# The rounded weight pieces start 64 bytes past a multiple of 256 instead of on one

## The chip, the cores and the metric

The kernel runs on one core of one Trainium2 chip. The metric is device time in microseconds (us) of one execution. Before the change three timed runs took 3041.02, 3044.77 and 3041.26 us; the median is 3041.26 us.

## The reference

The reference is one forward pass over 512 tokens of width 1024, in float32: a first block with four kinds of attention and a feed-forward part with a short convolution, then two layers of a second block. Cut to what matters here:

```python
def first_block(x, ...):                                  # once
    x = x + token_mixer(rmsnorm(x, norm_mix_g), ...)      # proj = xn @ w_in; four attentions; gates; @ w_out
    x = x + conv_ffn(rmsnorm(x, norm_ffn_g), ...)         # xn @ w_up (1024 x 5632), conv of width 3, @ w_down
    return rmsnorm(x, norm_final_g)

for l in range(2):                                        # second block
    h = h + 0.5 * swiglu(rmsnorm_2(h, ...), w_gate, w_up, w_down)       # 1024 x 2816, 1024 x 2816, 2816 x 1024
    z = rmsnorm_2(h, mix_norm[l]) @ w_in[l]
    y_a, y_b, y_c, y_d = mla(...), spatial_gating(...), hgrn2(...), retention(...)
    h = h + concatenate([y_a, y_b, y_c, y_d]) @ w_out[l]
    h = h + 0.5 * swiglu(rmsnorm_2(h, ...), w_gate, w_up, w_down)
    h = h + (p[l] @ ple_w_proj[l]) * sigmoid(rmsnorm_2(h, ...) @ ple_w_gate[l])
return rmsnorm_2(h, final_norm)
```

By far the most work is the product of the 512 tokens with weight matrices that are read from HBM once each.

## The kernel before

**Products in three terms.** A float32 value is split into a rounded part and the rest, both stored as float32r ("fp32r" in the trace, shown as f32 with TensorE's instructions). Activations `x` become `xh` and `xl`, weights become `wh` and `wl`. A product is then three matmuls that add up in one PSUM bank: `wh` with `xh`, `wh` with `xl` (both in a first loop over the chunks of 128 along the contraction), and `wl` with `xh` (in a second loop). In `products` these are lines 728, 729 and 737; `fm_steps` has them on lines 775, 776, 780 and 784, `grains_fm` on 850, 851 and 858, the down projection of `ffn` on 1269, 1270 and 1277.

**Who is stationary.** Nearly always the weights are stationary (128x128, loaded by a LDWEIGHTS ahead of each matmul) and 512 tokens stream past them. So each float32r matmul with 512 columns has its own weight load, which runs while the matmul before it still streams. In the token-major form (`token_major` and `grains_tm`, lines 808 to 885) it is the other way round: the activations are stationary and 256 columns of `wh` or `wl` stream.

**Pieces.** Weights come in pieces of 128x1024 float32 values (`PIECE`), two slots deep. The sync engine (SP) loads piece n into `raw[:, n % 2, :]`. GpSimd (POOL) writes `wh[:, n % 2, :]` from it in one instruction (line 678) and `wl[:, n % 2, :]` as raw minus wh in four (line 685). A slot of `wh` may be written again when TensorE's first loop over the piece before last is done (semaphore `rounded_read`), a slot of `wl` when its second loop is done (`pieces_used`). TensorE waits for `pieces_split`. The activations are in `xh`, `xl`, `op_hi`, `op_lo` or in the large tensor `arena` (seen as float32r under the name `arena_rounded`).

**Where things lie.** Tensors are allocated one behind the other, each start rounded up to a multiple of 32 bytes; every number here is bytes within a partition. What TensorE reads starts so:

| tensor | start | start mod 256 | read by TensorE as |
|---|---|---|---|
| `arena` | 18432 | 0 | both operands |
| `xh`, `xl`, `op_hi`, `op_lo` | 142592, 158976, 175360, 183552 | 0 | streamed, sometimes stationary |
| `const` | 199968 | 32 | both, plain float32 |
| `ident16`, `mask16` | 204096, 204352 | 64 | both, bf16 |
| `between` | 204640 | 96 | by nobody: it fills 160 bytes |
| `wh`, `wl` | 204800, 212992 | 0 | stationary; streamed in the token-major form |
| `ones` | 221568 | 128 | stationary, plain float32 |
| `nrm` | 223104 | 128 | stationary, four matmuls |

A chunk of 128 columns of a piece is 512 bytes, and so is the step between the chunks: where `wh` starts at a multiple of 256, each stationary operand in it does too. The streamed activations also step by multiples of 512 bytes.

**Other matmuls.** The attentions and mixers use plain float32 operands. The profile has two matmuls for each plain float32 one of the program. Those matter below which follow directly on a float32r stream: line 901 (`squares`, stationary `ones`), line 1490 (`mean_square`, stationary `const`), line 1312 (`rank_one`, stationary in `arena`), and line 1122 (`qk`, stationary in `arena`).

**What sets the order.** TensorE's order is written out by hand: the matmuls of the pieces are laid between those of the attentions and mixers. Nothing in it depends on addresses.

Of the kernel before, what the change touches and what calls it, by code (L numbers as in the profile page):

```python
# [30 lines left out]
P = 128  # L31
# [208 lines left out]
def program(nc, x, out, k, scratch, book):  # L240
# [3 lines left out]
    def sb(name, shape, dt=F32):  # L244
        return ctx.enter_context(nc.sbuf_tensor(name, shape, dt))
# [29 lines left out]
    const = sb("const", [P, CONST_N])  # L275

    ident16, mask16 = sb("ident16", [P, P], BF16), sb("mask16", [P, P + 2], BF16)
    sb("between", [P, 40])
    assert nc.sbuf_base % 256 == 0, nc.sbuf_base % 256
    wh, wl = sb("wh", [P, 2, PIECE], F32R), sb("wl", [P, 2, PIECE], F32R)  # L280
    lcol = sb("lcol", [P, LAYERS * L_NROWS])
    ones = sb("ones", [P, 3, P])
# [2975 lines left out]
def build(nc, arrays, known=None):  # L3258

    k = {n: nc.dram_tensor(f"in_{n}", a.shape, mybir.dt.from_np(a.dtype), kind="ExternalInput").ap()  # L3260
         for n, a in arrays.items()}
    out = nc.dram_tensor("out_0", (1, S, D), F32, kind="ExternalOutput").ap()
    scratch = nc.dram_tensor("t5_by_distance", (8, 640), F32).ap()
    book = Book(known)
    program(nc, k["x"][0], out[0], k, scratch, book)
    return book
# [20 lines left out]
```

## Time and profile before

| | |
|---|---|
| timed runs | 3041.02, 3044.77, 3041.26 us, median 3041.26 us |
| profiled execution | 3041.56 us, its span 3040.3 us |
| mean granted TensorE clock | 0.998 of full speed |
| TensorE matmuls | 14934, busy 3003.6 us (99%) |
| TensorE weight loads | 14934, busy 2432.5 us (80%) |
| POOL | busy 2176.3 us (72%) |
| VectorE (DVE), ScalarE (ACT) | busy 1415.7 us (47%), 724.5 us (24%) |
| DMA | 272.90 MB, mean 90 GB/s |

The span is the time from the first to the last instruction of the program; the profiled execution's own time is 1.3 us longer. In the trace a matmul's record begins when it begins to stream and ends when its result is modelled to be complete, so records overlap: a duration of 389 ns does not mean that the next matmul waits for 389 ns. The distance from start to start is what a matmul costs.

### The profile page before, as it was taken

How to read it: one execution, taken by the hardware profiler on the slowest of the kernel's cores; microseconds unless marked ns; L12 is line 12 of the kernel's file. 1: busy time of each engine (PE TensorE's matmuls, PEld its weight loads, DVE VectorE, ACT ScalarE, POOL GpSimd, SP SyncE). 2: the span in 40 equal slices, each digit the busy share in tenths (PEclk: the TensorE clock that was granted, in tenths of full speed). 3: DMA queues.
4: the chain of work that ended last, by engine and by line, in shares of the span. 5: the costliest groups of instructions: out<-in, count | busy, mean ns of one | idle time of the engine just before them, and what ended most of it. 6: DMA issues, size and time to landing. Idle time of an engine off the chain costs nothing.

```text
span 3040.3 us, 39415 instructions
## 1 busy us (share of the span) xinstructions
PE 3003.6 (99%) x14934; PEld 2432.5 (80%) x14934; DVE 1415.7 (47%) x2157; ACT 724.5 (24%) x1434; POOL 2176.3 (72%) x2524
## 2 busy tenths in 40 slices
PE   9999999999999999999999999999999999999998
PEld 7776777888888888887788888888888877888886
DVE  5467556777156421476732212622213767422214
ACT  3433222222021100344411101311002444111003
POOL 6665668988788877754487777877777554877775
PEclk9999999999999999999999999999999999999999
DMA  5322223333333333322133333333323221333332
GB/s 162 79 67 63 77 80 91 97 97 97 99 100 104 97 97 97 92 55 62 56 99 97 97 103 97 94 98 97 98 96 94 63 55 54 100 97 98 104 97 83
DMA packets 469205, 272.90 MB, mean 90 GB/s; under 512 B 20798, under 2 KB 465136, under 8 KB 469016
## 3 DMA queue, kind: packets, MB, share of 16 engines
q1 hardware_dynamic: 466904, 267.22, 29.7%
q10 hardware_dynamic: 2112, 3.17, 0.3%
q8 instruction: 118, 1.93, 0.3%
q14 instruction: 71, 0.58, 0.1%
HBM read 268.21 MB, written 2.12 MB: 89 GB/s over the span
## 4 chain that ended last, share of the span: by engine, by line
PE 86%; DVE 3%; ACT 1%; issue 0%; DVEq 0%; ACTq 0%
PE bank L728 17%; PE bank L729 17%; PE bank L737 17%; PE bank L1269 7%; PE bank L1277 7%; PE bank L1270 7%; PE bank L850 2%; PE bank L858 2%; PE bank L851 1%; PE bank L775 1%; PE bank L776 1%; DVE arena L2343 1%; PE bank L780 1%; PE bank L1122 1%; PE bank L1442 1%; PE bank L885 1%
## 5 line engine op out<-in xcount | busy, mean ns | idle before, releaser
L685 POOL TENSOR_TENSOR wl<-raw,wh 128x256 fp32r<-128x256 f32 x2016 | 1617.0, 832 | 286.0 <-PE bank L737 182.2
L678 POOL TENSOR_SCALAR wh<-raw 128x1024 fp32r<-128x1024 f32 x504 | 562.8, 1117 | 555.4 <-PE bank L729 170.2
L728 PE MATMUL bank<-xh,wh 128*128 128x512 f32 x1552 | 610.7, 393 | 0.0
L729 PE MATMUL bank<-xl,wh 128*128 128x512 f32 x1552 | 604.3, 389 | 0.0
L2343 DVE TENSOR_TENSOR arena<-bank,nrm 128x512 f32<-128x512 f32 x236 | 152.4, 685 | 541.9 <-PE bank L737 541.7
L737 PE MATMUL bank<-xh,wl 128*128 128x512 f32 x1552 | 390.6, 391 | 0.0
L2343 DVE TENSOR_TENSOR arena<-arena 128x512 f32<-128x512 f32 (+1 forms) x373 | 339.1, 915 | 59.5 <-ACT arena L2059 11.7
L728 PEld LDWEIGHTS bank<-xh,wh 128*128 128x128 f32 x1552 | 291.7, 188 | 62.7 <-issue 2.1
L737 PEld LDWEIGHTS bank<-xh,wl 128*128 128x128 f32 x1552 | 289.9, 188 | 64.6 <-issue 4.6
L729 PEld LDWEIGHTS bank<-xl,wh 128*128 128x128 f32 x1552 | 291.5, 188 | 60.4 <-issue 1.2
L728 PE MATMUL bank<-arena_rounded,wh 128*128 128x512 f32 x824 | 321.7, 390 | 1.0 <-DVE arena L2343 1.0
L729 PE MATMUL bank<-arena_rounded,wh 128*128 128x512 f32 x824 | 320.6, 389 | 0.0
L2352 DVE SCALAR_TENSOR_TENSOR h<-bank,h 128x512 f32<-128x512 f32 x64 | 44.3, 692 | 481.0 <-PE bank L1277 445.9
L1269 PE MATMUL bank<-arena_rounded,wh 128*128 128x512 f32 x592 | 230.7, 390 | 0.0
L1270 PE MATMUL bank<-arena_rounded,wh 128*128 128x512 f32 x592 | 230.3, 389 | 0.0
L1991 ACT ACTIVATE arena<-arena 128x512 f32<-128x512 f32 x88 | 55.7, 633 | 682.6 <-DVE arena L2343 682.6
L737 PE MATMUL bank<-arena_rounded,wl 128*128 128x512 f32 x824 | 203.5, 389 | 0.0
L728 PEld LDWEIGHTS bank<-arena_rounded,wh 128*128 128x128 f32 x824 | 154.7, 188 | 34.0 <-DVE arena L2343 1.4
L729 PEld LDWEIGHTS bank<-arena_rounded,wh 128*128 128x128 f32 x824 | 154.7, 188 | 32.4 <-issue 0.5
L737 PEld LDWEIGHTS bank<-arena_rounded,wl 128*128 128x128 f32 x824 | 154.7, 188 | 32.1
L1277 PE MATMUL bank<-arena_rounded,wl 128*128 128x512 f32 x592 | 161.5, 389 | 0.0
L1277 PEld LDWEIGHTS bank<-arena_rounded,wl 128*128 128x128 f32 x592 | 111.1, 188 | 23.2
(370 smaller groups left out, 4098.6 us busy)
## 6 DMA issues: line engine op xcount, KB each, us to landing
raw<-in_ffn_w_gate SPq DMA_DIRECT2D x176, 256.0 KB, 3.1
raw<-in_ffn_w_up SPq DMA_DIRECT2D x176, 256.0 KB, 3.1
raw<-in_ffn_w_down SPq DMA_DIRECT2D x176, 256.0 KB, 2.9
raw<-in_w_in SPq DMA_DIRECT2D x158, 256.0 KB, 3.1
raw<-in_w_up SPq DMA_DIRECT2D x88, 256.0 KB, 3.2
raw<-in_w_gate SPq DMA_DIRECT2D x64, 256.0 KB, 3.1
raw<-in_w_out SPq DMA_DIRECT2D x48, 256.0 KB, 3.0
raw<-in_w_down SPq DMA_DIRECT2D x44, 256.0 KB, 2.9
```

The source lines that it names most:

```text
L678: pool.tensor_scalar(wh[:, s, :], raw[:, s, :], 1.0, 0.0, ALU.mult, ALU.add).then_inc(split, 1)
L685: ins = pool.tensor_tensor(wl[:, s, c], raw[:, s, c], wh[:, s, c].bitcast(F32), ALU.subtract)
L728: pe.matmul(psum, cols(wh, i), xhi, start=(i == 0), stop=False)
L729: ins = pe.matmul(psum, cols(wh, i), xlo, start=False, stop=False)
L737: ins = pe.matmul(psum, cols(wl, i), xhi, start=False, stop=(i == last))
L850: pe.matmul(o, cols(wh, i), xhi, start=(i == 0), stop=False)
L858: ins = pe.matmul(o, cols(wl, i), xhi, start=False, stop=(i == last))
L1269: pe.matmul(bank[2 * s + b][:, :], w, xhi, start=(kk == 0 and i == 0), stop=False)
L1270: ins = pe.matmul(bank[2 * s + b][:, :], w, xlo, start=False, stop=False)
L1277: ins = pe.matmul(bank[2 * s + b][:, :], cols(wl, i, b), hid[2 * kk + i][0], start=False, stop=end)
L1991: act.activation(t, t, other_table(ACT.Silu)).then_inc(*A.up("silu", tag, n))
L2343: v.tensor_tensor(out, a, b, op).then_inc(*V.up(*what))
```

## The change

The filler `between` grows from 40 to 56 float32 values, that is by 64 bytes. All that is allocated behind it moves up by 64 bytes: `wh` (now at 204864, 64 past a multiple of 256), `wl` (at 213056, likewise 64 past), `lcol`, `ones` (now 192 past a multiple of 256) and `nrm` (likewise 192 past). Nothing ahead of it moves: `arena`, `xh`, `xl`, `op_hi`, `op_lo`, `raw` and `const` stay. The instructions of every engine, their order and their waits are the same as before.

```diff
     ident16, mask16 = sb("ident16", [P, P], BF16), sb("mask16", [P, P + 2], BF16)
-    sb("between", [P, 40])
-    assert nc.sbuf_base % 256 == 0, nc.sbuf_base % 256
+    sb("between", [P, 56])
+    assert nc.sbuf_base % 256 == 64, nc.sbuf_base % 256
     wh, wl = sb("wh", [P, 2, PIECE], F32R), sb("wl", [P, 2, PIECE], F32R)
     lcol = sb("lcol", [P, LAYERS * L_NROWS])
     ones = sb("ones", [P, 3, P])
```

## Rows read from the trace of the kernel before

**Rows 1.** Page: busy time of TensorE and POOL; the chain that ended last, by line.
```profile
PE 3003.6 (99%) x14934; PEld 2432.5 (80%) x14934; DVE 1415.7 (47%) x2157; ACT 724.5 (24%) x1434; POOL 2176.3 (72%) x2524
...
PE bank L728 17%; PE bank L729 17%; PE bank L737 17%; PE bank L1269 7%; PE bank L1277 7%; PE bank L1270 7%; PE bank L850 2%; PE bank L858 2%; PE bank L851 1%; PE bank L775 1%; PE bank L776 1%; DVE arena L2343 1%; PE bank L780 1%; PE bank L1122 1%; PE bank L1442 1%; PE bank L885 1%
```
**Rows 2.** Busy by stretch: stretch, length, then busy and count for each engine.
```profile
600.00:700.00 100.00, 100.00 (x442) 82.78 (x442) 73.08 (x75) 25.74 (x37) 88.26 (x92) 1.00 0.33 96
...
1020.00:1180.00 160.00, 160.00 (x707) 132.49 (x706) 38.47 (x47) 16.38 (x26) 120.32 (x147) 1.00 0.31 96
2010.00:2280.00 270.00, 270.00 (x1193) 223.58 (x1192) 66.23 (x83) 29.00 (x46) 202.35 (x248) 1.00 0.32 96
```
**Rows 3.** L728: count, duration ns least/median/most, first and last start.
```profile
L728 PE MATMUL bank<-xh,wh x1552: 387/389/798, 51.0 to 2604.3; 128*128 128x512 f32 x194
...
L728 PE MATMUL bank<-arena_rounded,wh x824: 389/389/798, 30.8 to 3023.6; 128*128 128x512 f32 x165
...
L728 PE MATMUL bank<-op_hi,wh x112: 389/392/504, 191.0 to 2603.9; 128*128 128x512 f32 x112
```
**Rows 4.** L1269: the same view.
```profile
L1269 PE MATMUL bank<-arena_rounded,wh x592: 387/389/481, 754.9 to 2966.6; 128*128 128x512 f32 x198
...
L1269 PE MATMUL bank<-op_hi,wh x160: 389/389/389, 749.4 to 2941.2; 128*128 128x512 f32 x160
...
L1269 PE MATMUL bank<-xh,wh x128: 389/389/389, 1776.1 to 2952.1; 128*128 128x512 f32 x128
```
**Rows 5.** Groups of PE: count | busy us, mean ns | idle before.
```profile
L850 PE MATMUL bank<-xh,wh 128*128 128x512 f32 x192 | 80.1, 417 | 0.4 <-ACT arena L2092 0.4
...
L775 PE MATMUL bank<-xh,wh 128*128 128x512 f32 x96 | 37.7, 393 | 2.6 <-DVE xl L2343 2.1 <-DVE xl L2352 0.5
```
**Rows 6.** One matmul each, L780 and L851, the last ahead of L901 and L1490.
```profile
L780 PE MATMUL bank<-xh,wl x1: 396/396/396, 519.8 to 519.8; 128*128 128x512 f32 x1
```
```profile
L851 PE MATMUL bank<-xl,wh x1: 397/397/397, 2477.9 to 2477.9; 128*128 128x512 f32 x1
```
**Rows 7.** One matmul each, L737 and L851, the last ahead of L1312 and L1122.
```profile
L737 PE MATMUL bank<-xh,wl x1: 389/389/389, 2329.8 to 2329.8; 128*128 128x512 f32 x1
```
```profile
L851 PE MATMUL bank<-xl,wh x1: 389/389/389, 2471.8 to 2471.8; 128*128 128x512 f32 x1
```
**Rows 8.** Timeline of PE: start us, length us; what follows the four matmuls above.
```profile
520.04 1.02 PE L901 MATMUL bank<-arena,ones 128*128 128x512 f32 x2
```
```profile
2478.14 1.02 PE L1490 MATMUL bank<-arena,const 128*128 128x512 f32 x2
```
```profile
2329.99 0.39 PE L1312 MATMUL bank<-const,arena 128*128 128x1 f32 x3
```
```profile
2471.99 0.38 PE L1122 MATMUL bank<-arena 96*128 96x128 f32 x2
```
**Rows 9.** Timeline of PE behind a group of transposes.
```profile
293.97 0.39 PE L729 MATMUL bank<-xl,wh 128*128 128x512 f32 x1
...
295.13 0.39 PE L728 MATMUL bank<-xh,wh 128*128 128x512 f32 x1
...
296.49 0.39 PE L728 MATMUL bank<-xh,wh 128*128 128x512 f32 x1
```
**Rows 10.** L1523 and L1338, plain float32 matmuls: least/median/most ns.
```profile
L1523 PE MATMUL bank<-arena,const x16: 592/592/646, 1403.4 to 2493.0; 128*128 128x512 f32 x16
```
```profile
L1338 PE MATMUL bank<-arena,const x8: 592/592/648, 1385.0 to 2462.2; 128*128 128x512 f32 x8
```
**Rows 11.** L876, token-major: `wh` streams, 256 columns.
```profile
L876 PE MATMUL bank<-wh,xh x256: 277/283/387, 76.5 to 2499.9; 128*128 128x256 f32 x128
```
**Rows 12.** POOL's groups: count | busy us, mean ns | idle us before.
```profile
L685 POOL TENSOR_TENSOR wl<-raw,wh 128x256 fp32r<-128x256 f32 x2016 | 1617.0, 832 | 286.0 <-PE bank L737 182.2 <-PE bank L858 52.5 <-PE bank L885 29.2
L678 POOL TENSOR_SCALAR wh<-raw 128x1024 fp32r<-128x1024 f32 x504 | 562.8, 1117 | 555.4 <-PE bank L729 170.2 <-PE bank L1270 145.2 <-PE bank L877 77.9
```

## The prediction

> **What bounds the kernel now.** I read the page first, then busy time by stretch, then single lines of TensorE with their least, median and longest durations, and last the timeline around the places where float32r matmuls meet others. On the page the reader is to see that matmuls are under way for 99% of the span and that three quarters of the chain that ended last are six lines, the three terms of a product in `products` and in the down projection [rows 1]. So the end is set by how fast TensorE can begin one matmul after another. The stretches give that pace: 442, 707 and 1193 matmuls in 100, 160 and 270 us, 226 to 227 ns each, at full clock, with VectorE busy between a quarter and three quarters of the time [rows 2]. The pace does not react to VectorE. At 2.4 GHz, the clock granted there, 512 columns take 213.3 ns. So each matmul carries 13 ns beyond its columns.
>
> These 13 ns are what the change can touch, since it moves no instruction and no wait, only the address of the stationary operand of most matmuls. How many are concerned: L728 has 1552 + 824 + 112 = 2488 [rows 3], L1269 592 + 160 + 128 = 880 [rows 4], L850 192 and L775 at least 96 [rows 5]: 3656, and each has two partners (the other terms), so 10,968 matmuls with 512 columns and a weight load each. Smaller groups of the same kind, some 500, are left out. **One nanosecond more or less for each is 11.0 us, or 0.36%.** Nothing else in this kernel has such a lever.
>
> All streamed activations start at a multiple of 256 in these rows, be it in `xh` (256 past a multiple of 512) or in `arena` (0 past it). The median is 389 ns for both [rows 3, 4]: a shift of 256 between the two operands changes nothing. What a shift of 64 does no float32r row shows. I bound it.
>
> **Part 1, the stationary operand moves by 64 bytes.** The trace has one natural experiment. A weight load runs beside the matmul ahead of it. Where a float32r stream ends and a plain float32 matmul follows, the last stream runs beside a load from another tensor. Ahead of L901 (stationary `ones`, 128 past a multiple of 256) that last matmul lasts 396 ns, ahead of L1490 (stationary in `const`, 32 past one) 397 ns [rows 6, 8]. Ahead of L1312 and L1122, whose stationary operands lie in `arena` at a multiple of 256, the same kind of matmul lasts 389 ns, the median of all [rows 7, 8]. I read durations here because the end is modelled from the pace: a longer one goes with a later next start. So two offsets on either side of 64, namely 32 and 128, cost 7 to 8 ns, and offset 0 costs nothing. That is the nearest row to the change.
>
> Against taking it whole: these are single matmuls at a change of kind, not a stream in which every load is shifted. And the cost isn't a function of the addresses alone. Behind transposes the float32r stream runs with unchanged alignment, but its first matmuls come slower: from 293.97 to 295.13 are five distances, 1.16 us or 232 ns each; from 295.13 to 296.49 six, 1.36 us or 227 ns each [rows 9]. The stream finds its steady pace after some five matmuls. With the loads shifted it may settle at another pace. The unsettled distances are 5 ns over the settled ones, the shifted loads 7 ns. I take 6 ns, between the two: 10,968 x 6 = 66 us. The ends: 0 if the stream settles to the old pace, 8 ns or 88 us if every matmul pays what the one ahead of L1490 pays, 100 us if those left out pay it too; and below nothing, next.
>
> Downwards: the fastest matmuls of L728 and L1269 last 387 ns, 2 ns under the median [rows 3, 4], so -22 us is a pace that occurs. A farther bound comes from plain float32, which streams a column in two cycles: 592 ns for 512 columns [rows 10]. That is 203 ns more than 389, where the columns alone take 213.3 ns more. So a plain float32 matmul carries 10 ns less beside its load. If the shift took away all that the float32r stream has on top, it would be 10 x 10,968 = 110 us less.
>
> **Part 2, `wh` and `wl` as the streamed operand.** Token-major matmuls last 283 ns in the median, 277 at least [rows 11]; with 256 columns each, L876 and its partners L877 and L885 are 768. For a streamed operand off its place I have plain float32 only: L1338 streams from 160 past a multiple of 256, L1523 from a multiple of 256, and both have 592 ns [rows 10]. I take 0. With 8 ns each it would be 6 us, with -6 ns it would be -5 us.
>
> **Part 3, POOL.** It writes `wh` and `wl` 64 bytes farther on. One piece costs POOL 1117 + 4 x 832 = 4445 ns [rows 12]; TensorE uses a piece for 24 matmuls, 24 x 227 = 5450 ns. So 1.0 us for each piece is idle, and POOL's idle time, 286 + 555 us, is mostly ended by TensorE giving a slot back [rows 12]. Any change of under a fifth in POOL's writes stays hidden. If the cover were gone, TensorE would wait at each of the 504 pieces. `lcol`, `ones` and `nrm` move too; `ones` was off a multiple of 256 already (128, now 192). I take 0 for both.
>
> **Sum.** 3041.6 us for the profiled execution (its span 3040.3 and 1.3 around it), plus 66 us, is 3108 us. That execution is 0.3 us above the median of the runs, so I leave it at 3108.
>
> **Rival 1: nothing changes, 3041 us.** The steady pace would be the same for any shift that keeps whole lines of memory. For it: a shift by 256 does nothing, POOL and VectorE do nothing to the pace, and the stream returns to it after each disturbance [rows 2 to 4, 9]. Against: the 7 to 8 ns [rows 6]. The Trainium skill supports this rival ("TensorE: Matmul & The Clock Gate", step by step, LDWEIGHTS): the streamed operand and the weight load have two independent read ports, so a load takes no bandwidth from the running matmul. By that rule addresses could not matter, and 396 against 389 ns would have to come from something else in the change of kind, such as the two passes of a plain float32 matmul; L1312, also plain float32 with stationary operand at a multiple of 256, speaks against that. The same section gives 216 ns for bf16 matmuls of 512 columns one after another; this trace has 227 for float32r with a load each.
>
> **Rival 2: faster.** The extra 13 ns are not fixed: they differ by 5 ns with the same addresses [rows 9], so a part is two readers getting into each other's way, and plain float32 at half the rate of columns is spared 10 of them. Had the two operands started in the same place of the memory's interleaving so far, 64 bytes would pull them apart. The small form is the pace of the fastest rows, 3041 - 22 = 3019 us; the large one takes the 10 ns away, 3041 - 110 = 2931 us. Against: 32 and 128 are apart as well and cost more, not less.
>
> **Rival 3: slower by POOL.** If a shifted start broke up POOL's accesses and its instructions grew by more than 23%, POOL would set the pace: at 30% more, a piece would take 5.78 us instead of 5.45, and 504 of them 166 us more, 3207 us. Nothing in the trace speaks for it, as all starts stay at multiples of 64.
>
> **How the numbers follow.** The forecast, slower by the shifted loads, gets 0.52: two rows agree, but they are single matmuls. No change gets 0.22. Faster gets 0.24, half of it the small form, half the large one or what lies between. POOL gets 0.02. The likeliest case's own range is 3060 (2 ns) to 3145 us (the 100 us above and a few for part 2). For 8 in 10 I take 3005 to 3150: this leaves out half of the faster cases, the POOL case and little above. Under 0.2%, some 6 us, is what a measurement of this kernel can't tell from no change; on each side of it: faster 0.24, same 0.22, slower 0.54.
>
> **What would show it.** In the profile after, busy time by stretch between 2010 and 2280 us would hold 1150 to 1170 matmuls instead of 1193, and the median of L728 would be 394 to 397 ns instead of 389, that of L1523 592 as before. With rival 1 the medians stay at 389; with rival 2 they fall to 387 or to about 379. With rival 3 they stay and TensorE waits for POOL's L678 and L685. I am wrong if the stream settles: then only the matmuls behind a change of kind differ. The matmul ahead of L901 is a further test: its load moves from 128 to 192 past a multiple of 256, and ahead of L1312 a load at a multiple of 256 now runs beside a stream whose own load was shifted.

## The result and the profile after

The kernel after takes 3109.73 us in the median (3108.87 to 3111.62, four runs); the kernel before took 3041.14 us beside it (3040.90 to 3044.77, four runs). The ratio is 1.0224, with a 95% interval of 1.0206 to 1.0241: slower by 68.6 us. The forecast was 3108 us, in a range of 3005 to 3150.

The profiled execution took 3111.62 us, its span 3110.3 us, 70.0 us more than before, at a granted clock of 0.997. The page shows the same number of instructions; only TensorE's busy time has grown with the span, by 70.5 us against [rows 1]:

```profile
PE 3074.1 (99%) x14934; PEld 2433.0 (78%) x14934; DVE 1412.0 (45%) x2157; ACT 724.3 (23%) x1434; POOL 2162.8 (70%) x2524
```

The same three stretches as in [rows 2] (stretch, length, then busy time and count for PE, PEld, DVE, ACT and POOL, then the granted clock, the DMA share and GB/s):

```profile
600.00:700.00 100.00, 100.00 (x430) 80.13 (x430) 70.88 (x72) 24.89 (x36) 84.64 (x90) 1.00 0.32 95
1020.00:1180.00 160.00, 160.00 (x688) 128.92 (x687) 40.64 (x51) 16.39 (x26) 116.11 (x143) 1.00 0.31 95
2010.00:2280.00 270.00, 270.00 (x1159) 217.58 (x1158) 72.28 (x91) 29.71 (x47) 198.74 (x244) 1.00 0.32 95
```

430, 688 and 1159 matmuls stand where there were 442, 707 and 1193. That is 232.6, 232.6 and 233.0 ns for each instead of 226.2, 226.3 and 226.3, at the same full clock: 6.2 to 6.6 ns more (one matmul more or less in a count is 0.5 ns in the shortest stretch and 0.2 ns in the longest). It is so in a stretch in which VectorE is busy for 71% of the time and in one where it is 25%, so how busy VectorE is does not matter here.

The float32r lines, with least, median and longest duration, against [rows 3, 4]:

```profile
L728 PE MATMUL bank<-xh,wh x1552: 392/394/802, 50.8 to 2662.6; 128*128 128x512 f32 x194
...
L728 PE MATMUL bank<-arena_rounded,wh x824: 393/398/801, 30.6 to 3093.6; 128*128 128x512 f32 x165
...
L728 PE MATMUL bank<-op_hi,wh x112: 392/398/505, 191.7 to 2662.1; 128*128 128x512 f32 x112
```
```profile
L1269 PE MATMUL bank<-arena_rounded,wh x592: 393/394/481, 769.2 to 3035.3; 128*128 128x512 f32 x198
```

The fastest matmul of line 728 with `xh` now (392) is slower than its median was (389). Plain float32 matmuls, against [rows 10], have not moved, and the token-major ones, against [rows 11], are shorter:

```profile
L1523 PE MATMUL bank<-arena,const x16: 592/592/647, 1433.9 to 2550.2; 128*128 128x512 f32 x16
```
```profile
L876 PE MATMUL bank<-wh,xh x256: 276/279/393, 76.3 to 2557.1; 128*128 128x256 f32 x128
```

What happened is best seen where a float32r stream starts. The place of [rows 9], behind the same transposes, looks so in the timeline of the kernel after (start us, length us):

```profile
297.29 0.40 PE L729 MATMUL bank<-xl,wh 128*128 128x512 f32 x1
...
299.63 0.40 PE L729 MATMUL bank<-xl,wh 128*128 128x512 f32 x1
...
300.56 0.40 PE L729 MATMUL bank<-xl,wh 128*128 128x512 f32 x1
```

From 297.29 to 299.63 are ten distances, 234 ns each, and from 299.63 to 300.56 four, 232 ns. Before, the stream ran at 232 ns for five matmuls and then fell to 227. Now it starts near that pace and never falls: it is the pace in the middle of a long stretch too (2088.27 to 2090.14 are eight distances, 1.87 us or 234 ns each):

```profile
2088.27 0.39 PE L729 MATMUL bank<-xl,wh 128*128 128x512 f32 x1
...
2090.14 0.39 PE L729 MATMUL bank<-xl,wh 128*128 128x512 f32 x1
```

Five is not a fixed number. Behind other transposes of the kernel before, the stream needed ten distances to settle (98.14 to 100.44 us, 2.30 us or 230 ns each, and 227 to 228 from there on), and behind some only two (from 363.13 us).

```profile
98.14 0.39 PE L729 MATMUL bank<-xl,wh 128*128 128x512 f32 x1
...
100.44 0.39 PE L729 MATMUL bank<-xl,wh 128*128 128x512 f32 x1
```

POOL, against [rows 12], has more idle time than before and slightly shorter instructions:

```profile
L685 POOL TENSOR_TENSOR wl<-raw,wh 128x256 fp32r<-128x256 f32 x2016 | 1610.5, 830 | 318.6 <-PE bank L737 213.5 <-PE bank L858 53.0 <-PE bank L885 30.5
L678 POOL TENSOR_SCALAR wh<-raw 128x1024 fp32r<-128x1024 f32 x504 | 555.3, 1102 | 606.0 <-PE bank L729 201.4 <-PE bank L1270 162.8 <-PE bank L877 76.9
```

### The profile page after: what moved, and what is told of

It is laid out like the page before. It is cut to its first block, busy times and chain, and to the rows that moved or that the text cites. A ratio compares the mean times of both kernels' runs of the same rounds, so it can differ in the third digit from the quotient of the medians.

```text
span 3110.3 us, 39415 instructions
## 1 busy us (share of the span) xinstructions
PE 3074.1 (99%) x14934; PEld 2433.0 (78%) x14934; DVE 1412.0 (45%) x2157; ACT 724.3 (23%) x1434; POOL 2162.8 (70%) x2524
## 4 chain that ended last, share of the span: by engine, by line
PE 94%; DVE 4%; ACT 1%; issue 0%; DMA 0%; DVEq 0%; SPq 0%; ACTq 0%
PE bank L728 19%; PE bank L737 18%; PE bank L729 18%; PE bank L1269 7%; PE bank L1277 7%; PE bank L1270 7%; PE bank L850 2%; PE bank L858 2%; PE bank L851 1%; DVE arena L2343 1%; PE bank L775 1%; PE bank L776 1%; PE bank L1122 1%; PE bank L920 1%; PE bank L780 1%; PE bank L885 1%
## 5 line engine op out<-in xcount | busy, mean ns | idle before, releaser
L685 POOL TENSOR_TENSOR wl<-raw,wh 128x256 fp32r<-128x256 f32 x2016 | 1610.5, 830 | 318.6 <-PE bank L737 213.5
L678 POOL TENSOR_SCALAR wh<-raw 128x1024 fp32r<-128x1024 f32 x504 | 555.3, 1102 | 606.0 <-PE bank L729 201.4
L728 PE MATMUL bank<-xh,wh 128*128 128x512 f32 x1552 | 619.9, 399 | 0.0
L729 PE MATMUL bank<-xl,wh 128*128 128x512 f32 x1552 | 613.5, 395 | 0.0
L737 PE MATMUL bank<-xh,wl 128*128 128x512 f32 x1552 | 400.1, 396 | 0.0
L728 PEld LDWEIGHTS bank<-xh,wh 128*128 128x128 f32 x1552 | 292.2, 188 | 71.8 <-issue 1.4
L737 PEld LDWEIGHTS bank<-xh,wl 128*128 128x128 f32 x1552 | 289.9, 188 | 74.0 <-issue 4.6
L728 PE MATMUL bank<-arena_rounded,wh 128*128 128x512 f32 x824 | 327.6, 398 | 0.8 <-DVE arena L2343 0.8
L729 PE MATMUL bank<-arena_rounded,wh 128*128 128x512 f32 x824 | 324.3, 394 | 0.0
L1269 PE MATMUL bank<-arena_rounded,wh 128*128 128x512 f32 x592 | 234.2, 396 | 0.0
L1270 PE MATMUL bank<-arena_rounded,wh 128*128 128x512 f32 x592 | 233.8, 395 | 0.0
L737 PE MATMUL bank<-arena_rounded,wl 128*128 128x512 f32 x824 | 208.9, 395 | 0.0
L728 PEld LDWEIGHTS bank<-arena_rounded,wh 128*128 128x128 f32 x824 | 154.6, 188 | 40.3 <-DVE arena L2343 1.2
L737 PEld LDWEIGHTS bank<-arena_rounded,wl 128*128 128x128 f32 x824 | 154.6, 188 | 37.7
L1277 PE MATMUL bank<-arena_rounded,wl 128*128 128x512 f32 x592 | 165.3, 395 | 0.0
```

The costliest lines, as they stand in the source:

```text
L678: pool.tensor_scalar(wh[:, s, :], raw[:, s, :], 1.0, 0.0, ALU.mult, ALU.add).then_inc(split, 1)
L685: ins = pool.tensor_tensor(wl[:, s, c], raw[:, s, c], wh[:, s, c].bitcast(F32), ALU.subtract)
L728: pe.matmul(psum, cols(wh, i), xhi, start=(i == 0), stop=False)
L729: ins = pe.matmul(psum, cols(wh, i), xlo, start=False, stop=False)
L737: ins = pe.matmul(psum, cols(wl, i), xhi, start=False, stop=(i == last))
L1269: pe.matmul(bank[2 * s + b][:, :], w, xhi, start=(kk == 0 and i == 0), stop=False)
```

## The experiments

Three theories stood against each other. Theory 1: what counts is how far the stationary operand starts from the streamed one, modulo 256 bytes. Theory 2: the stationary operand's own place counts. Theory 3: every operand off a multiple of 256 has its price. All diffs are against the kernel before. An inserted tensor that nobody reads moves all that lies behind it; one of 16 float32 values moves it by 64 bytes. Asserts that state an address change with it and are mostly left out of the diffs.

### All operands 64 bytes on (e1_all64)

```diff
+    sb("ahead", [P, 16])                         # ahead of arena: all of the table moves by 64 bytes
-    assert arena_at % 256 == 0, arena_at % 256
+    assert arena_at % 256 == 64, arena_at % 256
```

> 64 bytes are put ahead of arena and the filler between stays at 40, so that arena, xh, xl, op_hi, op_lo, raw, const, wh, wl, ones and nrm all begin 64 bytes farther on: the streamed and the stationary operand both start 64 past a multiple of 256. Theory 1 (what counts is the offset between the two operands): 3041 us, the steady matmul of L728 389 ns, as before the change. Theory 2 (what counts is the stationary operand's own place against a multiple of 256): 3110 us, 394 ns, as after the change. Theory 3 (every operand off its place costs by itself): above 3110 us, up to 3175.

Measured: 3046.44 us (3042.19 to 3048.13, ten runs) against 3042.61; ratio 1.0010 (1.0001 to 1.0019). The stretch and line 729, here line 730:

```profile
2010.00:2280.00 270.00, 270.00 (x1193) 223.64 (x1192) 64.38 (x80) 26.51 (x42) 203.10 (x248) 1.00 0.32 98
```
```profile
L730 PE MATMUL bank<-xl,wh x1552: 387/389/628, 53.4 to 2609.9; 128*128 128x512 f32 x194
```

With both operands at 64 the pace is that of both at 0. Theories 2 and 3 fall for the stream with 512 columns: `wh` and `wl` are exactly where the kernel after has them, and the 68 us are not there. Some 4 us are, and the stream is not where they arise. In the profile the down projection, line 1270 here, has its first start 4.1 us later than in [rows 4], and its last, 2.2 ms on, only 5.3 us later:

```profile
L1270 PE MATMUL bank<-arena_rounded,wh x592: 387/389/476, 759.0 to 2971.9; 128*128 128x512 f32 x198
```

Most of the 4 us goes with the granted clock. In the profile of this run the clock is 0.91 in three stretches of 20 us, 265 to 285, 1345 to 1365 and 2425 to 2445 us; in that of the kernel before it is 0.91 in the second alone. The first of them, in the kernel before and then in this run:

```profile
265.00:285.00 20.00, 19.33 (x106) 13.62 (x105) 14.03 (x44) 7.50 (x20) 9.20 (x12) 1.00 0.14 41
```
```profile
265.00:285.00 20.00, 19.34 (x105) 14.19 (x103) 15.63 (x48) 6.41 (x17) 8.16 (x11) 0.91 0.12 36
```

As an estimate from these rows, 9% of 20 us is 1.8 us for each of the two more. In the timed runs it is alike: six of the ten had a mean clock of 0.996 (3045.95 to 3048.13 us), where three of 19 of the kernel before had (3044.55 to 3045.13); its two runs at 0.998 took 3042.19 and 3043.13 us, nine of the kernel before at 0.998 took 3040.87 to 3042.73. Whether the shifted addresses have a part in the lower clock stays open.

### Only the streams 64 bytes on (e2_streams64)

```diff
+    sb("ahead", [P, 16])
-    sb("between", [P, 40])
+    sb("between", [P, 24])                       # wh and what follows stay where they were
```

> The streamed operands alone move: arena, xh, xl, op_hi, op_lo begin 64 past a multiple of 256, wh and wl stay at the very address of before (between is 24 long). Theory 1: the offset between the operands is 64 again, with the other sign, so the time leaves 3041 us; if the sign doesn't matter 3110 us, if it does anything from 2990 to 3150, and the same as with the stationary operand 192 past and the streams at a multiple of 256. Theory 2: 3041 us, 389 ns. Theory 3: about 3110 us.

Measured: 3064.39 us (3063.58 to 3065.41, four runs), ratio 1.0071 (1.0056 to 1.0086); 1181 matmuls in the long stretch, 228.6 ns each, median 392 ns. `wh` and `wl` haven't moved, and the time has, so their own place is not what counts. (`raw`, `const` and the bf16 tensors moved with the streams; the pace of the long stretch, where only float32r matmuls run, is not theirs.) But the price is 22 us, not 68: with the stationary operand 64 bytes ahead of the streamed one, modulo 256 that is 192 behind, the stream is better off than with it 64 behind.

### Only `wl` 64 bytes on (e3_wl64)

```diff
-    wh, wl = sb("wh", [P, 2, PIECE], F32R), sb("wl", [P, 2, PIECE], F32R)
+    wh = sb("wh", [P, 2, PIECE], F32R)
+    sb("amid", [P, 16])
+    wl = sb("wl", [P, 2, PIECE], F32R)
```

> 64 bytes between wh and wl: wh stays at a multiple of 256, wl, lcol, ones and nrm begin 64 bytes farther on. One of three products has a shifted stationary operand. If the cost belongs to each matmul whose load is shifted: a third of 69 us, 3064 us, with L737 at 394 ns and L728 at 389. If the stream as a whole has to find a pace and a run of unshifted loads keeps it: L737 below 394 ns and the time under 3055 us.

Measured: 3076.11 us (3074.65 to 3078.87), ratio 1.0109 (1.0093 to 1.0126). One term of three is shifted, and half of the cost is there. Both branches of the expectation missed: the time is neither 3064 us nor under 3055, though the medians of line 737 (394 ns) and 728 (389) are those of the first. The timeline shows where the rest is (lines 730, 731 and 739 are 728, 729 and 737 of the kernel before):

```profile
2054.93 2.03 PE L739 MATMUL bank<-xh,wl 128*128 128x512 f32 x8
2056.79 0.39 PE L730 MATMUL bank<-xh,wh 128*128 128x512 f32 x1
...
2058.18 0.39 PE L730 MATMUL bank<-xh,wh 128*128 128x512 f32 x1
...
2060.45 1.80 PE L739 MATMUL bank<-xh,wl 128*128 128x512 f32 x7
```

The eight matmuls of line 739 take 1.86 us to the next start, 232.5 ns each. Behind them `wh` is stationary, unshifted, and still the first six distances are 232 ns (2056.79 to 2058.18, 1.39 us); the ten from 2058.18 to 2060.45 are 227. So each shifted group leaves a stretch to settle behind it. In the down projection, groups of four shifted matmuls stand between eight unshifted ones, and of those eight six are slow again (796.59 to 797.98, 1.39 us or 232 ns each): the median of line 1271 (1269 before) is 393 ns though neither of its operands has moved.

```profile
796.59 0.39 PE L1271 MATMUL bank<-arena_rounded,wh 128*128 128x512 f32 x1
...
797.98 0.39 PE L1271 MATMUL bank<-arena_rounded,wh 128*128 128x512 f32 x1
```
```profile
L1271 PE MATMUL bank<-arena_rounded,wh x592: 389/393/481, 760.5 to 3000.9; 128*128 128x512 f32 x198
```

### 64 bytes behind `wl` (e4_tail64)

```diff
     wh, wl = sb("wh", [P, 2, PIECE], F32R), sb("wl", [P, 2, PIECE], F32R)
+    sb("behind_wl", [P, 16])
```

> 64 bytes behind wl: wh and wl stay, only lcol, ones and nrm begin 64 bytes farther on. If the stationary weights are all of the cause: 3041 us. If the norms' operands had a part in it (ones streams or is stationary in 18 program matmuls, nrm is read by VectorE's multiplications): a part of the 69 us shows here, over 3047 us.

Measured: 3042.73 us (ten runs), ratio 0.9998 (0.9989 to 1.0007), 1193 matmuls in the long stretch. `lcol`, `ones` and `nrm`, which moved with `wh` and `wl` in the change, are worth nothing that can be told from the noise.

### The distance swept, in steps of 32 bytes

These keep the streams at multiples of 256 and set the start of `wh` and `wl` by the length of `between`: 48 values for 32 bytes, none for 96, 8 for 128, 24 for 192, 32 for 224, 16 for 160. `lcol`, `ones` and `nrm` move along; that this is worth nothing was measured for 64 bytes alone.

```diff
-    sb("between", [P, 40])
+    sb("between", [P, 48])                       # s_w32; 8 in s_w128, 16 in s_w160, 24 in s_w192, 32 in s_w224
```
```diff
-    sb("between", [P, 40])                       # s_w96: between is left out
```

At 32 (s_w32): 

> wh and wl begin 32 past a multiple of 256 (between is 48 long), the streams stay at multiples. The last stream ahead of L1490, whose load was 32 past, cost 7 to 8 ns more in the kernel before. If that holds for every load: about 3110 to 3120 us, L728 at 394 to 397 ns. If 64 is a place of its own: 3041 us.

At 96 (s_w96): 

> wh and wl begin 96 past a multiple of 256 (no filler). If any offset costs the same: 3110 us. If two readers meet by their distance in a pattern of 256 bytes, the cost differs from that of 64: anything from 3041 to 3150 us.

At 128 (s_w128): 

> wh and wl begin 128 past a multiple of 256. The last stream ahead of L901, whose load was 128 past, cost 7 ns more. If that holds for every load: 3110 us; if the pattern has a period of 128 bytes: 3041 us.

At 192 (s_w192): 

> wh and wl begin 192 past a multiple of 256, the mirror of 64. Theory 1 (offset between the operands): the same time as with the streams alone 64 past a multiple, whatever that is. Theory 2 (the stationary operand's own place): about 3110 us, while the streams alone gave 3041.

The distances 32, 96 and 128 took 3109.6, 3119.5 and 3103.6 us: the whole cost at each, so the pattern does not repeat after 128 bytes.

The long stretch of the run at 192:

```profile
2010.00:2280.00 270.00, 270.00 (x1181) 221.53 (x1181) 66.83 (x83) 27.77 (x44) 202.40 (x246) 1.00 0.32 96
```

3061.20 us and 1181 matmuls, where e2_streams64 had 3064.39 us and 1181. The streams 64 on and the weights 64 back are the same distance, and they give the same pace, the same median (392 ns) and the same token-major median (276 ns). With e1_all64 this shows that the distance decides.

### Two finer steps, and the rest of the sweep

For 16 and 240 bytes, which the allocation's steps of 32 don't give, one tensor holds both, and its views begin 16 bytes in:

```diff
-    wh, wl = sb("wh", [P, 2, PIECE], F32R), sb("wl", [P, 2, PIECE], F32R)
+    w = sb("w", [P, 4 * PIECE + 8], F32R)        # s_w16; in s_w240 between has 32 values as well
+    wh, wl = (w[:, a:a + 2 * PIECE].rearrange("p (s c) -> p s c", s=2) for a in (4, 2 * PIECE + 4))
```

In these last four expectations theories 1 and 2 stand for narrower rivals, which each spells out. Where they speak of pieces and rounded halves, it is `wh` and `wl` alone that move; `raw` stays.

At 16 (s_w16): 

> Pieces and rounded halves begin 16 bytes behind multiples of 256 (one tensor holds both, its views begin 16 bytes in), the streams at multiples of 256. Theory 1 (the pace hangs on how far the stationary operand begins behind the streamed one): if the distance counts down to 16 bytes, as it does from 32 on, some 3110 us with 394 to 395 ns for a matmul of L728 and 1159 matmuls from 2010 to 2280 us. Theory 2 (only whole steps of 32 bytes or more count, and 16 bytes are the same place as 0): 3042 us, 389 ns, 1193 matmuls. Something between would say that the cost rises with the distance near 0.

At 240 (s_w240): 

> Pieces and rounded halves begin 16 bytes ahead of a multiple of 256 (240 behind), the streams at multiples of 256. Theory 1: 192 behind took 3061 us; on the way back to 0 the cost goes to nothing or stays at 20 us: 3042 to 3061 us, 389 to 392 ns, 1181 to 1193 matmuls from 2010 to 2280 us; far from the 3110 us of 32 behind, as the cost is one-sided. Theory 2 (any place off the streams' own costs alike near it): some 3110 us, 394 ns, 1159 matmuls.

At 224 (s_w224): 

> Pieces and rounded halves begin 224 bytes behind multiples of 256, the streams at multiples of 256. Theory 1: between the kernel before and 192 behind (3061 us), 3042 to 3061 us, 389 to 392 ns, 1181 to 1193 matmuls from 2010 to 2280 us. Theory 2 (every place off 0 within 64 bytes costs the whole): 3110 us. A time below 3041 us, with a matmul of L728 under 389 ns, would say that 0 is not the best distance.

At 160 (s_w160): 

> Pieces and rounded halves begin 160 bytes behind multiples of 256, the streams at multiples of 256; the last of the eight distances in steps of 32 bytes. Measured so far: 0 3042 us, 16 3092, 32 3110, 64 3110, 96 3119, 128 3104, 192 3061, 224 3110, 240 3050. Theory 1 in its form that the cost falls evenly from 128 (3104) to 192 (3061): 3083 us, 393 ns, 1170 matmuls from 2010 to 2280 us. Theory 2, that every distance off 0 costs about the same and 192 alone is cheap among the multiples of 32 (224 behind had the full cost): 3104 to 3110 us, 394 ns or more, 1159 matmuls.

All distances together (start of `wh` modulo 256, streams at 0; ratio to the kernel before as timed beside each, 3041.14 to 3042.61 us; matmuls between 2010 and 2280 us):

| start | us | ratio, 95% interval | matmuls |
|---|---|---|---|
| 0 (before) | 3041.1 | 1 | 1193 |
| 16 | 3092.2 | 1.0165 (1.0145 to 1.0185) | 1159 |
| 32 | 3109.6 | 1.0222 (1.0192 to 1.0251) | 1159 |
| 64 (after) | 3109.7 | 1.0224 (1.0206 to 1.0241) | 1159 |
| 96 | 3119.5 | 1.0254 (1.0224 to 1.0284) | 1154 |
| 128 | 3103.6 | 1.0202 (1.0172 to 1.0231) | 1159 |
| 160 | 3112.2 | 1.0229 (1.0209 to 1.0250) | 1159 |
| 192 | 3061.2 | 1.0069 (1.0046 to 1.0092) | 1181 |
| 224 | 3109.7 | 1.0221 (1.0201 to 1.0241) | 1159 |
| 240 | 3050.0 | 1.0027 (1.0017 to 1.0037) | 1193 |

After 128 and 192, I had added to theory 1 that the cost was one-sided and would fall evenly on the way from 128 back to 0. The runs at 224 (3110, not 3042 to 3061) and at 160 (3112, not 3083) refute that. What stands is: 0 costs nothing, 192 costs 20 us, the other multiples of 32 cost 62 to 78 us; 16 and 240 lie between (at 240 the long stretch is as before, but 703 matmuls stand between 1020 and 1180 us instead of 707). None of the distances tried beats 0. Why 192 is cheap and both of its neighbours are not stays open.

The run at 16 bytes adds how the cost arises. Its stretches are not slower by a part; they are of two kinds:

```profile
1020.00:1180.00 160.00, 160.00 (x707) 132.55 (x706) 37.92 (x48) 15.15 (x24) 119.44 (x146) 1.00 0.33 98
2010.00:2280.00 270.00, 270.00 (x1159) 218.64 (x1158) 66.94 (x85) 27.80 (x44) 196.66 (x242) 1.00 0.32 94
```

707 matmuls in the first, as in the kernel before; 1159 in the second, as in the kernel after. The matmuls are of the same lines with the same tensors, line 737 with `xh` for example, eight in a row in each stretch:

```profile
1041.76 1.98 PE L737 MATMUL bank<-xh,w 128*128 128x512 f32 x8
```
```profile
2103.03 2.03 PE L737 MATMUL bank<-xh,w 128*128 128x512 f32 x8
```

Less the 0.39 us of the last one, that is seven distances of 227 and of 234 ns. With the same distance between the operands the stream settles in one place and does not in the other. What decides this stays open.

## Why the prediction was right, step by step

**The bound and the lever.** Right. Three quarters of the chain were float32r matmuls one after another, and the change came from their pace. The count was low by the 500 matmuls of smaller groups that the prediction left out.

**Part 1, 6 ns for each shifted load.** Right in direction and size: 6.2 to 6.6 ns in the stretches, 68.6 us in all, 6.3 ns for each of 10,968. What it is a cost of is shown too, and it is not quite what the prediction said. It spoke of the place of the stationary operand; with the streams at a multiple of 256 that is the same number as the distance between the operands, and only e1_all64 and e2_streams64 tell the two apart: the distance counts. That it came out within 2 us is in part luck. The 6 ns were chosen between single matmuls with 7 to 8 ns [rows 6], which proved a weak sign (next paragraph), and unsettled distances with 5 ns [rows 9], whose like lasted two to ten matmuls in other places of the same kernel. And nothing in the argument tells 64 bytes from 192: it would have given about the same 3108 us there, where 3061 was measured. Where the stream had no time to settle before, there was little to lose. That, and the token-major gain, is the likely reason for 68.6 us where 10,968 and 500 matmuls by 6.4 ns would be 73; no run splits the difference.

**The tests at the changes of kind.** The last matmul ahead of line 1490 lasted 397 ns before [rows 6] and now lasts 392, though line 1490's stationary operand hasn't moved; the last one ahead of line 1312 lasted 389 [rows 7] and is now among those with 394 to 397. The one ahead of line 901, which the prediction named as a further test, went from 396 to 393 ns, 1 ns under the median of the kernel after. So the duration of such a matmul tells the state of the stream at that moment at least as much as the address of the load beside it. The "natural experiment" pointed the right way, but it was weaker than it looked.

```profile
L851 PE MATMUL bank<-xl,wh x1: 392/392/392, 2535.1 to 2535.1; 128*128 128x512 f32 x1
```
```profile
L737 PE MATMUL bank<-xh,wl x2: 394/396/397, 2383.8 to 2384.1; 128*128 128x512 f32 x2
```
```profile
L780 PE MATMUL bank<-xh,wl x1: 393/393/393, 527.3 to 527.3; 128*128 128x512 f32 x1
```

**Part 2, token-major.** Forecast at nothing; it is a small gain. The median duration falls from 283 to 279 ns, the distance from start to start by less. Sixteen matmuls of line 885 in a row, less the 0.28 us of the last, have fifteen distances of 120 ns before and 117 after:

```profile
80.38 2.08 PE L885 MATMUL bank<-wl,xh 128*128 128x256 f32 x16
```
```profile
80.17 2.04 PE L885 MATMUL bank<-wl,xh 128*128 128x256 f32 x16
```

For 768 of them that is some 2 us. The sign was missed, because the price of a shifted stream was taken from plain float32. Here too the distance decides: with both operands 64 on (e1_all64) the median is 283 again, with the streams alone 64 on it is 276. For 256 columns with a load each, distance 0 is no optimum.

**Part 3, POOL, `ones`, `nrm`.** Right. POOL has more idle time than before (318.6 + 606.0 against 286.0 + 555.4 us), and e4_tail64 shows the tail to be worth nothing.

**Rival 1, no change,** fails in the medians and in the time. Its support was the rule of the Trainium skill ("TensorE: Matmul & The Clock Gate", step by step, LDWEIGHTS) that stream and weight load have independent read ports. The measurement decides against what was drawn from it: same instructions, same loads, only another address, and 6.4 ns for each matmul. The runs show that the pace depends on the two addresses together; that the two readers meet in the memory is the reading that fits this, but no run shows it directly.

**Rival 2, faster,** fails for 512 columns at all nine distances off 0 that were tried: in none does the long stretch hold more matmuls than before. Its premise, that the old distance was the bad one, was upside down. For 256 columns it was right.

**Rival 3, POOL,** fails: its instructions became no longer (830 and 1102 ns against 832 and 1117).

**The signs.** 1159 matmuls in the long stretch (forecast 1150 to 1170), 592 ns for line 1523 as forecast, and for line 728 a median of 394 ns with `xh` (forecast 394 to 397), 398 with `arena` and `op_hi`.

**The range.** With 3005 to 3150 it was far wider than the error of 2 us. The sweep shows that a wide range was fair: the nine distances off 0 cost from 7 to 78 us, and the rows before gave no means to tell them apart.

## What to carry to other kernels

Where float32r matmuls follow on each other with a weight load each, put the streamed and the stationary operand at the same offset modulo 256 bytes; here every multiple of 32 but 192 costs 2.0 to 2.5% of the kernel, and a common shift by 64 costs 0.1%, most of which goes with the clock. An insertion of a small tensor ahead of the weights can so cost more than most edits gain, with an unchanged instruction list: when a time moves and no instruction did, compare the counts of matmuls in a long stretch, then the operands' addresses. And look in the timeline at how a stream begins: a pace that is found only after some matmuls can be lost, and its first matmuls give a rough size of what that would cost.

## What the runs showed of the hardware

- The pace of float32r matmuls (512 columns, a load each, granted clock 1.00) depends on the distance of the operands' starts modulo 256 bytes, with the same instructions. In the long stretch it is 226.3 ns at 0, 228.6 ns at 192, 233.0 ns at 32, 64, 128, 160 and 224, and 234.0 ns at 96. At 16 and 240 bytes it depends on the place in the program too.
- At distance 0 a stream needs some matmuls behind a disturbance to reach the fast pace: five behind the transposes of [rows 9], two to ten behind others, six behind shifted loads (e3_wl64).
- The token-major form (256 columns) has its longest median, 283 ns, at distance 0, and at 96 too; its shortest, 276 ns, at 192.
- Plain float32 matmuls with 512 columns stay at 592 ns for 160 and 0 bytes of the stream's start [rows 10], before and after.
